# A shared value projection in seven block products, in a fused two-layer transformer kernel

## The reference, cut to what matters

```python
def rmsnorm(x, g):
    xf = x.astype(jnp.float32)
    y = xf * lax.rsqrt(jnp.mean(xf * xf, axis=-1, keepdims=True) + EPS)
    return (y * g.astype(jnp.float32)).astype(x.dtype)
...
x = x + jax.nn.sigmoid(x @ ple_w_gate[i]) * (p[i] @ ple_w_proj[i])
if i == N_A - 1:
    kv = rmsnorm(x, kv_ln_g) @ w_kv_shared
    k_sh = kv[..., :MIX_WIDTH].reshape(B, S, N_HEADS, HEAD_DIM).transpose(0, 2, 1, 3)
    v_sh = kv[..., MIX_WIDTH:].reshape(B, S, N_HEADS, HEAD_DIM).transpose(0, 2, 1, 3)
```

## Time and profile before

| what | value |
|---|---|
| median of 3 runs | 1315.89 us (1315.56 to 1316.05) |
| span of the profiled execution, first to last instruction | 1314.1 us |
| TensorE | busy 1295.6 us, 99% of the span |
| VectorE | busy 758.1 us, 58% |
| ScalarE | busy 642.3 us, 49% |
| GpSimd | busy 343.7 us, 26% |

### The profile page before, as it was taken

How to read it: one execution, slowest core, us unless ns; L and a number is a source line. 1 busy time by engine, 2 the same in 40 slices (tenths; PEclk the granted TensorE clock), 3 DMA queues, 4 the chain that set the end, 5 groups by cost and what they waited for, 6 DMA issues and landing times.

```text
span 1314.1 us, 17855 instructions
## 1 busy us (share of the span) xinstructions
PE 1295.6 (99%) x6478; PEld 1086.5 (83%) x6478; DVE 758.1 (58%) x1209; ACT 642.3 (49%) x1164; POOL 343.7 (26%) x393
## 2 busy tenths in 40 slices
PE   7999999999999999999999999999999999999998
PEld 6998778788888888888888888889888888888986
DVE  5656889735652226898444653335467335578843
ACT  5379888624432325998244433414234234355632
POOL 2238877400000007773000000000000000668620
PEclk9999999999999999999999999999999999999999
DMA  5332100132232232001323333332332421421121
GB/s 192 84 108 65 45 25 15 53 106 97 81 99 97 99 99 73 17 0 32 112 97 93 87 93 97 96 97 64 87 110 82 135 96 49 129 65 49 33 64 65
DMA packets 70867, 104.66 MB, mean 80 GB/s; under 512 B 3476, under 2 KB 31368, under 8 KB 70664
## 3 DMA queue, kind: packets, MB, share of 16 engines
q1 hardware_dynamic: 69584, 99.44, 24.3%
q0 software_dynamic: 1088, 4.17, 1.1%
q10 hardware_dynamic: 120, 0.05, 0.0%
HBM read 101.55 MB, written 2.10 MB: 79 GB/s over the span
## 4 chain that ended last, share of the span: by engine, by line
PE 89%; DVE 5%; issue 3%; ACT 2%; DMA 1%; SPq 0%; DVEq 0%; POOL 0%; ACTq 0%; POOLq 0%
PE ps L496 24%; PE ps L498 23%; PE ps L497 23%; PE ps L700 3%; PE ps L1006 2%; PE ps L858 2%; PE ps L713 1%; PE ps L950 1%; PE ps L679 1%; PE ps L727 1%; PE ps L848 1%; DVE sp L2086 1%; PE ps L849 1%; PE ps L728 1%; DVE sp_l L2091 1%
## 5 line engine op out<-in xcount | busy, mean ns | idle before, releaser
L1689 DVE TENSOR_TENSOR w_lo<-stage,w_hi 128x1024 fp32r<-128x1024 f32 (+4 forms) x188 | 224.1, 1192 | 415.1 <-ACT w_hi L1108 414.9
L1108 ACT ACTIVATE w_hi<-stage 128x1024 fp32r<-128x1024 f32 (+4 forms) x188 | 191.0, 1016 | 457.2 <-PE ps L498 456.8
L496 PE MATMUL ps<-a0h,w_hi 128*128 128x512 f32 x512 | 204.5, 399 | 1.1 <-DVE q_lo L2273 0.8
L498 PE MATMUL ps<-a0h,w_lo 128*128 128x512 f32 x512 | 199.9, 390 | 0.0
L497 PE MATMUL ps<-a0l,w_hi 128*128 128x512 f32 x512 | 199.5, 390 | 0.0
L2375 POOL TENSOR_TENSOR small<-small 128x16 f32<-128x16 f32 (+2 forms) x14 | 32.3, 2311 | 388.0 <-DVE small L1767 284.4
L496 PE MATMUL ps<-w_hi,a0h 128*128 128x512 f32 (+1 forms) x320 | 121.9, 381 | 0.1
L498 PE MATMUL ps<-w_hi,a0l 128*128 128x512 f32 (+1 forms) x320 | 119.9, 375 | 0.0
L497 PE MATMUL ps<-w_lo,a0h 128*128 128x512 f32 (+1 forms) x320 | 119.8, 374 | 0.0
L496 PEld LDWEIGHTS ps<-a0h,w_hi 128*128 128x128 f32 x512 | 96.2, 188 | 20.5 <-DVE w_lo L1689 1.3
L498 PEld LDWEIGHTS ps<-a0h,w_lo 128*128 128x128 f32 x512 | 96.1, 188 | 20.6
(11 more groups left out here) (330 smaller groups left out, 2840.0 us busy)
## 6 DMA issues: line engine op xcount, KB each, us to landing
stage<-in_a_w_in SPq DMA_DIRECT2D x48, 512.0 KB, 3.7
stage<-in_ple_w_gate SPq DMA_DIRECT2D x16, 512.0 KB, 3.3
stage<-in_w_kv_shared SPq DMA_DIRECT2D x16, 512.0 KB, 3.6
stage<-in_sb_w_in SPq DMA_DIRECT2D x16, 512.0 KB, 3.7
stage<-in_a_w_out SPq DMA_DIRECT2D x16, 512.0 KB, 3.4
stage<-in_b_w_in SPq DMA_DIRECT2D x16, 512.0 KB, 3.7
stage<-in_mla_w_in SPq DMA_DIRECT2D x8, 512.0 KB, 3.9
stage<-in_sb_w_out SPq DMA_DIRECT2D x8, 512.0 KB, 3.4
```

The costliest lines, as they stand in the source:

```text
L496: pe.matmul(bank, wh, mh, start=start and not seeded, stop=False, skip_group_check=seeded)
L498: return pe.matmul(bank, wl, mh, start=False, stop=stop, skip_group_check=seeded)
L1108: act.activation(slab(w_hi[r % 2], L, nk, w), slab(stage[r % 4], L, nk, w), ACT.Copy).then_inc(S("hi_ready"), 1)
L1689: dve.tensor_tensor(slab(w_lo[r % 2], L, nk, w), slab(stage[r % 4], L, nk, w), slab(w_hi[r % 2], L, nk, w), ALU.subtract)\
```

## The change

The value product is a 2 x 2 block product: activations (512 tokens x 1024 features) in four blocks of 256 tokens x 512 features, weight in four blocks of 512 features x 512 columns (b11, b12, b21, b22). Eight block products become seven, with sums of blocks as operands:

- t1 = b12 - b11, t3 = b22 - b12, t2 = t1 - b22 (in place), t4 = b21 + t2 (in place). GpSimd makes them from the staged float32 blocks, in halves of 128 x 1024: eight operations (`weight_sums`).
- Four sums of activation blocks, made by GpSimd from the residual and the gain: four gain products and four sums of 128 x 1024 (`times_gain`, `total`), then split by ScalarE (`sums_hi`) and VectorE (`sums_lo`).

Each product is called a step here (0 to 6, in the order of `SPLITS`). It takes two pairs of feature tiles; a pair (0 to 13) is 2 tiles x 2 output tiles x 3 = 12 matmuls of 128 x 512 and takes one slot of the same two-slot ring. Steps 0 and 4 use banks a, step 2 b, steps 1 and 5 c, steps 3 and 6 d, two banks each; b and a are the banks of the first group, c and d those of the second, from which VectorE first reads the key. Step 4 adds to a, 5 to c and 6 to d what is already there, after ScalarE or VectorE has read it. The outputs are put together from the banks with twelve adds on VectorE (semaphore `sums_out`) and six scaled reads on ScalarE (`first_out`).

The stages' count of slots is now kept in tables (`stage_of`, `ring_need`), since the four blocks use three pairs of stage buffers and two buffers of their own. The four input loads at the start share one semaphore instead of four. The core of the diff:

```diff
-        Linear("sh_v", w_sh, 8, columns(D, 2 * D), True, A0, items("h_kv")),
+        Linear("sh_v", w_sh, 8, columns(D, 2 * D), True, A0, items("h_kv"), fast=Fast(sv_slots, (s_hi, s_lo))),
...
+            for j in range(Fast.N):
+                ring_need[L.load0 + j] = L.load0 + j - 1
...
+        def load_fast(L):
+            for name, p, to, src, landed, need in L.fast.order:
+                if need:
+                    sp_.wait_ge(S("lo_ready"), need)
+                if name == "b21":
+                    sp_.wait_ge(S("t_ok"), p + 1)
+                sp_.dma_start(to[:, :, :], src).then_inc(landed[0], 16)
...
-        linear("sh_v")
+        def fast(L):
...
+            steps = (("a", act(0, 0)), ("c", total(2)), ("b", total(1)), ("d", total(0)), ("a", act(4, 0)), ("c", total(3)), ("d", act(4, T // 2)))
+            pe.wait_ge(S(group_read[G - 2][0]), group_read[G - 2][1])
+            for n, (to, a) in enumerate(steps):
+                if n == 1:
+                    pe.wait_ge(S(group_read[G - 1][0]), group_read[G - 1][1])
+                    pe.wait_ge(S("s_lo"), 2)
+                if n == 2:
+                    pe.wait_ge(S("s_lo"), 4)
+                if n == 4:
+                    pe.wait_ge(S("first_out"), 4)
+                if n == 5:
+                    pe.wait_ge(S("sums_out"), 8)
+                for k in range(4):
+                    r = L.load0 + 2 * n + k // 2
+                    pe.wait_ge(S("lo_ready"), r + 1)
...
+                    for m in range(2):
+                        sl = slice(m * P, (m + 1) * P)
+                        mm = three(banks[to][m][:, :], a[k][0][:, sl], a[k][1][:, sl], wh, wl, k == 0 and n < 4, k == 3,
+                                   seeded=n >= 4)
+                    if k % 2:
+                        mm.then_inc(S("ring_used"), 1)
...
+            if L.fast:
+                src, name, p = L.fast.source(k0)
+                if name[0] == "t":
+                    act.wait_ge(S("t_ok"), {"t1": 1, "t3": 3, "t2": 5, "t4": 7}[name] + p)
+                else:
+                    act.wait_ge(*L.fast.landed[name, p])
+                act.wait_ge(S("ring_used"), ring_need[r])
+                act.activation(pair_slot(w_hi, r), src, ACT.Copy).then_inc(S("hi_ready"), 1)
+                return
...
+                if between:
+                    for n in range(4):
+                        reads(count - 1, [n], i)
+                        split_to(end + 2 + min(n, 1), i)
+                    return
...
+                if j == 10:
+                    dve.wait_ge(S(done), 6)
+                    for m in range(2):
+                        add(t[:, 2 + m, two], c[m], 2 + m, t[:, 2 + m, two], done)
...
+            for p in range(2):
+                pool.wait_ge(S("lo_ready"), L.load0 + 2 + p + 1)
+                n += 1
+                chunk_sum(home["t", p], home["t", p], home["b22", p], ALU.subtract, n)
+            for p in range(2):
+                pool.wait_ge(*landed["b21", p])
+                pool.wait_ge(S("lo_ready"), L.load0 + 8 + p + 1)
+                n += 1
+                chunk_sum(home["b21", p], home["b21", p], home["t", p], ALU.add, n)
...
+        pool.wait_ge(S("x_new"), 12)
+        times_gain(0, 0, T // 2, "h_kv")
+        link(times_gain(1, 0, 0, "h_kv"))
+        pool.wait_ge(S("x_new"), 16)
+        link(times_gain(2, 4, T // 2, "h_kv"))
+        total(2, 0, 2, ALU.add).then_inc(S("s_ok"), 1)
+        pool.wait_ge(S("s_ok"), 1)
+        total(0, 1, 0, ALU.subtract).then_inc(S("s_ok"), 1)
+        total(1, 1, 2, ALU.subtract).then_inc(S("s_ok"), 1)
         root(nrm, MB, "nrm_in", 2, "nrm_ok")
-        pool.wait_ge(S("x_new"), 16)
+        link(times_gain(3, 4, 0, "h_kv"))
+        pool.wait_ge(S("s_ok"), 3)
+        total(3, 3, 1, ALU.add).then_inc(S("s_ok"), 1)
+        pool.wait_ge(S("rstd_done"), 2)
+        weight_sums(lin["sh_v"], 0)
```

More of the change, by code:

```diff
@@ L383, in build @@
     group_read = []
+    stage_free, ring_need, stage_of, n_stage = [0] * 4, {}, {}, 0
+    loaded = [S(f"loaded{s}") for s in range(4)]
     for L in LINEARS:
@@ L389, in build @@
             group_read.append((L.read, L.read0 + 4 * (g + 1)))
-            if L.by_tile:
+            if L.fast:
+                L.lpg = Fast.N // 2
+                loads += [(L, g * L.lpg + j, 2, c0, w) for j in range(L.lpg)]
+            elif L.by_tile:
                 for c in range(c0, c0 + w, P):
@@ L401, in build @@
                     loads.append((L, k0, min(2, L.kt - k0), c0, w))
+        if L.fast:
+            L.fast.order = []
+            for name in ("b11", "b12", "b22", "b21"):
+                for p in range(2):
+                    r0, c0 = 4 * (name[1] == "2") + 2 * p, L.groups[name[2] == "2"][0]
+                    src = L.w[r0 * P:(r0 + 2) * P, c0:c0 + T].rearrange("(k p) n -> p k n", p=P)
+                    if name == "b12":
+                        to, landed, need = L.fast.extra[p], (S("b12_in"), 32), None
+                    else:
+                        q = n_stage % 4
+                        to, landed, need = stage[q], (loaded[q], 16 * (n_stage // 4 + 1)), stage_free[q]
+                        j = {"b11": 0, "b22": 10, "b21": 12}[name] + p + 1
+                        stage_free[q] = L.load0 + j
+                        n_stage += 1
+                    L.fast.home[name, p], L.fast.landed[name, p] = to, landed
+                    L.fast.order.append((name, p, to, src, landed, need))
+                L.fast.home["t", 0], L.fast.home["t", 1] = L.fast.extra[2:4]
+            for j in range(Fast.N):
+                ring_need[L.load0 + j] = L.load0 + j - 1
+        else:
+            for r in range(L.load0, len(loads)):
+                q = n_stage % 4
+                stage_of[r] = q, n_stage // 4 + 1, stage_free[q]
+                stage_free[q] = r + 1
+                n_stage += 1
         n_groups += L.n
@@ L427, in slab @@
         return t[:, 0:nk, 0:w]
-    loaded = [S(f"loaded{s}") for s in range(4)]
     block = ctx.enter_context(nc.Block())
@@ L630, in do @@
                     pe.wait_ge(S("act_lo"), 2)
-                    for m in range(MB):
-                        pe.wait_ge(S(f"x_in{m}"), 16)
+                    pe.wait_ge(S("x_in"), 16 * MB)
                 for k in range(a, b):
@@ L818, in _, with act, total @@
         linear("sh_k", 1)
-        linear("sh_v")
+        def fast(L):
+            G = L.group0
+            here, there = ps[4 * (G % 2):4 * (G % 2) + 4], ps[4 * (1 - G % 2):4 * (1 - G % 2) + 4]
+            banks = {"a": here[0:2], "b": here[2:4], "c": there[0:2], "d": there[2:4]}
+            hi, lo = L.fast.sums
+            def act(k0, t0):
+                return [tuple(t[:, t0:t0 + T // 2] for t in L.acts[k]) for k in range(k0, k0 + 4)]
+            def total(q):
+                return [(hi[:, q, k, :], lo[:, q, k, :]) for k in range(4)]
+            steps = (("a", act(0, 0)), ("c", total(2)), ("b", total(1)), ("d", total(0)), ("a", act(4, 0)), ("c", total(3)), ("d", act(4, T // 2)))
[13 more added lines that the diff above has]
+                    pe.wait_ge(S("lo_ready"), r + 1)
+                    wh, wl = pair_slot(w_hi, r)[:, k % 2, :], pair_slot(w_lo, r)[:, k % 2, :]
+                    for m in range(2):
[4 more added lines that the diff above has]
+                        mm.then_inc(S("ring_used"), 1)
+        fast(lin["sh_v"])
+        pe.wait_ge(S("first_out"), 6)
         linear("sb_gate")
@@ L1708, in group_done, with linear @@
             dve.wait_ge(S("ring_used"), L.load0 + (g + 1) * L.lpg + (0 if i is None else i * 2 * L.lpg))
-        def linear(name, read=None, extra=(), then=None, first=None, further=False, near=False):
+        def linear(name, read=None, extra=(), then=None, first=None, further=False, near=False, between=False):
             L, extra = lin[name], list(extra)
@@ L2074, in _, with sums_lo, do @@
         rest_of_layer(0, 1, "h_kv")
-        linear("sh_k", normed_to(kT_sh, 1), [nothing, nothing, norm(1, 1e-6, "sh_k")] + [lo_two("h_sb", t) for t in range(4)])
-        linear("sh_v")
+        def sums_lo(qs):
+            def do():
+                for n, q in qs:
+                    dve.wait_ge(S("s_hi"), n)
+                    dve.wait_ge(S("s_ok"), (2, 4, 3, 4)[q])
+                    dve.tensor_tensor(s_lo[:, q, :, :], s_f[:, q, :, :], s_hi[:, q, :, :], ALU.subtract).then_inc(S("s_lo"), 1)
+            return do
@@ L2077, in _ @@
+        linear("sh_k", normed_to(kT_sh, 1), [nothing, nothing, norm(1, 1e-6, "sh_k")] + [lo_two("h_sb", t) for t in range(3)]
+               + [lambda: (lo_two("h_sb", 3)(), sums_lo(((1, 2), (2, 0)))()), sums_lo(((3, 1), (4, 3)))], between=True)
+        fast_tokens(lin["sh_v"], v_sh)
         linear("sb_gate", normed_to(sg, 1))
```

126 lines of the change are left out of this document (115 added, 11 removed).

## The result

The changed kernel takes 1341.37 us (median of 4 runs, 1340.76 to 1342.22) against 1315.97 before: a ratio of 1.0193, 95% interval 1.0179 to 1.0208, or 25.4 us slower. The forecast was slower, at 1334, with a range of 1319 to 1340: right in direction, and the time lies just above the range.

The account below looks back on a forecast made before the run. TensorE, busy 1295.6 of 1314.1 us, was taken as the bound. Waits of 2.3 + 8.6 + 3.8 + 3.8 + 2.5 + 2.7 less 5.4 for removed matmuls gave 18.3 us, added to 1315.9: 1334 us, range 1319 to 1340.

Parts of the forecast that it names:

- matmuls removed: Value projection: seven products of 24 matmuls replace 192 matmuls, taking 24 x 0.227 = 5.4 us off TensorE.
- gate projection: Before the norm: two GpSimd gain products delay VectorE's split to 335.9 against 333.6, a TensorE wait of 2.3 us.
- norm, first half: Shared key projection: VectorE alternates with four GpSimd operations, so the token sums start at 364.2, a wait of 8.6 us.
- norm, second half: After the token sums: a gain product and a sum delay VectorE's diagonal, so the spreading matmul waits 3.8 us.
- head of the value projection: Step 1 waits 3.8 us for key bank reads; GpSimd's first four weight sums cost 2.5 us more by pair 1.
- pairs: Value projection: last two weight sums delay splits 0.7 us each, step 5 waits 1.3 for outputs; together 2.7 us.
- clock: TensorE falling to half clock after long waits: nothing in the forecast sum, up to 3 us in the first rival.
- first rival: TensorE's clock falls after the 8.6 and 3.8 us waits; sign: 0.63 us matmuls; 1334 + 3 = 1337 us; chance 0.12.
- The 18.4 us of turns: Key projection's end to pair 1's split: GpSimd's four weight sums (9.0) and VectorE's splits (9.4) alternate.
- the turns: VectorE operations reading two SBUF tensors run after GpSimd's, not beside; each that waited takes 0.14 us less than alone.
- The second (no hindrance, 1320): VectorE and GpSimd do not hinder each other; only instruction order costs, 3.7 us in sum, so 1320 us; chance 0.12.
- The third (not slower): GpSimd's wide sums take at most 1.23 us each, so the root is in time; 1315.6 us; chance 0.06.

Follow-up runs that it names:

- needless products: Changed kernel with 92 needless 128x512 matmuls on TensorE, placed ahead of its five long waits; 1337.4 us.
- the run with halves: Changed kernel with each of GpSimd's 16 gain products and sums written as two of 128x512 in place of one of 128x1024; 1334.1 us.
- the fills: Changed kernel with GpSimd's eight token gain products and sums each replaced by two constant fills, the token sums left out; 1332.9 us.
- The two best: Changed kernel with GpSimd's sums, root and VectorE's rests reordered (1318.9 us); the same with the rests of the tokens' sums made one by one (1319.1 us).

## Why the prediction came out where it did

| step | predicted | in the trace of the changed kernel |
|---|---|---|
| matmuls removed | -5.4 | -5.4 (24 instructions fewer) |
| gate projection | 2.3 | 1.7 |
| norm, first half | 8.6 | 8.1 |
| norm, second half | 3.8 | 3.4 |
| head of the value projection | 3.8 + 2.5 | 4.7 (step 1) + 3.6 (pair 0) |
| pairs | 2.7 | 0.7 + 2.1 (pair 9, step 5) |
| clock | 0 (3 in the first rival) | 5.4 + 0.8 (token sums) |
| sum | 18.3 | 25.1 |

The waits are distances of starts less 0.227 (at the token sums less the 0.45 of the kernel before); the norm's second half is the delay over the 3.76 us of the earlier trace rows, 4.2, less the 0.8 of the token sums at half clock. The right-hand sum stands against 25.4 measured.

*The step that failed* is the one that left TensorE's clock out of the likeliest case and priced it too low in the first rival, with the words that "no wait after the start is long enough to test it". It gave that case 0.12 and 3 us: one loss hidden in the wait for the diagonal and at most two more, after waits of 8.6 and 3.8 us. The fall came where no row had tested it, in the norm and at three other places: behind pair 0, step 1 and step 5, after waits of 3.4, 4.5 and 2.0 us. The norm's own fall was hidden in the wait for the diagonal, as the rival said, but for the 0.8 us of the token sums. The needless products show that the 5.4 us at the other places are a loss of their own and not a shadow of the waits. The start of the kernel had shown what matmuls at half clock cost; that should have been charged to every wait of several us in the sum. With the falls at these three places in it, the sum would have been near 1340 (1334 + 5.4).

*The second miss is a size:* the head, 8.3 in place of 6.3. Step 1 was priced "with no dispute about ports", and there was one: the split of pair 3 meets a block sum and takes 2.08 in place of 1.23, which is the 0.9 between 3.8 and 4.7. Pair 0's wait was taken as 2.5 between 1 and 4, near the case of loads that land in 3.6 us, 18 us ahead of the key projection's end. In the trace GpSimd's first block sum, released by a load, starts at 387.21, 11.3 us ahead of it (398.5):

```profile
387.21 5.75 POOL L2696 TENSOR_TENSOR sv_slot<-sv_slot,stage 128x1024 f32<-128x1024 f32 x2 [14.60 <-DMA sv_slot<-in_w_kv_shared]
...
409.11 2.35 POOL L2696 TENSOR_TENSOR sv_slot<-sv_slot,stage 128x1024 f32<-128x1024 f32 x1 [10.52 <-DVE w_lo L1835]
...
410.46 2.08 DVE L1835 TENSOR_TENSOR w_lo<-sv_slot,w_hi 128x1024 fp32r<-128x1024 f32 x1 [0.90 <-ACT w_hi L1217]
```

The 18.4 us of turns from there to the end of pair 1's split held (387.21 to 405.34).

*What held:* the turns, their price and their places. A GpSimd sum alone takes 2.39, as worked out from the earlier trace rows, a gain product 1.90 (2.26 forecast). A split beside them takes 1.7 to 3.4. The rule of the Trainium skill (SBUF — State Buffer, Who interferes with whom) is that a VectorE instruction with two SBUF inputs contends with a GpSimd instruction that reads SBUF, not with one that only writes it, and that the second to come waits for the whole of the first. Both halves of it agree: 1.5 to 1.8 us in place of 2.4 to 2.8 in the run with halves, and the 0.68 and 1.22 us beside the fills. The pairs came to 2.8 against 2.7, though with 0.7 once and 2.1 at step 5 in place of 0.7 twice and 1.3.

*The rivals.* The second (no hindrance, 1320) is refuted by VectorE's durations beside GpSimd's sums (2.38 to 3.35 us), which the fills for the token sums bring back to 0.68 to 1.22. The third (not slower) needed GpSimd sums of 1.23 us, and they take 2.39. The first was right in kind, and its sign, matmuls of 0.63 us after the waits, was seen.

*Open:* whether some order with whole sums gets below 1315.9. The two best gave 1318.9 and 1319.1, with the waits at different pairs.

## What to carry to other kernels

Work that is moved to GpSimd with two SBUF operands is not beside VectorE's own work of that kind but in one queue with it: add up both engines' durations over the stretch, and only then ask whether there is room. Here 16 sums of 1.9 to 2.4 us paid for 24 matmuls of 0.227. And a sum over waits in front of TensorE needs a second column, the matmuls that run at 1.2 GHz behind each long wait (here 1.5 to 2.3 us behind each of three waits of 2.0 to 4.5 us).
